# Sparse attention: projections as split products in one pass over the input, index scores of two heads side by side, index weights turned

## The reference, cut to what matters

```python
proj = h @ w_in                      # h: 512 x 1024, the normalised and modulated input
q = proj[..., :1024]                 # 16 heads of 64
ckv = _rmsnorm(proj[..., 1024:1152], kv_norm)     # latent, 128 wide
q_idx = proj[..., 1152:1664]         # 8 index heads of 64
k_idx = proj[..., 1664:1728]         # one index key of 64
w_idx = proj[..., 1728:] * (8 ** -0.5 * 64 ** -0.5)   # 8 weights a token
s = einsum('bthd,bsd->bths', q_idx, k_idx)
score = einsum('bth,bths->bts', w_idx, relu(s))   # causal; then the best 128 of each row
...                                  # attention over the selected latents, a bias by distance
```

## Time and profile before

| what | us |
|---|---|
| median of 3 runs | 2845.82 (2843.67 to 2848.26) |
| the profiled execution, own time | 2844.33 |
| its span, first to last instruction | 2842.5 |
| TensorE busy, share of span | 2707.7 (95%) |
| VectorE / ACT / POOL busy | 1369.2 / 1038.4 / 343.4 |
| mean granted TensorE clock | 0.978 |

### The profile page before, as it was taken

One profiled execution on the slowest core, in us unless ns is written; L12 is line 12 of the kernel. 1 busy time (PEld: TensorE's weight loads), 2 busy tenths in 40 slices (PEclk: granted clock), 3 DMA queues, 4 the chain that ended last, 5 costly groups with the idle time before them and its releaser, 6 DMA issues.

```text
span 2842.5 us, 46206 instructions
## 1 busy us (share of the span) xinstructions
PE 2707.7 (95%) x19024; PEld 2007.3 (71%) x19024; DVE 1369.2 (48%) x2302; ACT 1038.4 (37%) x1598; POOL 343.4 (12%) x268
## 2 busy tenths in 40 slices
PE   7999998899999989989999989999889999999999
PEld 4566666468888644577888868888677667788886
DVE  6566656253333337754333354433447676344335
ACT  5334333144432231744442243232223574333223
POOL 3232323010000101401000020000013131000000
PEclk9999999889999999999999989999989999999999
DMA  5344433322232112022223212232231002222231
GB/s 227 104 132 134 139 126 110 108 82 103 90 119 89 63 45 74 1 89 74 103 89 117 91 45 103 89 120 84 82 112 67 2 9 97 89 89 103 102 113 59
DMA packets 46585, 261.12 MB, mean 92 GB/s; under 512 B 5161, under 2 KB 7609, under 8 KB 26201
## 3 DMA queue, kind: packets, MB, share of 16 engines
q1 hardware_dynamic: 45416, 254.23, 25.8%
q10 hardware_dynamic: 1008, 4.57, 0.4%
HBM read 256.63 MB, written 2.15 MB: 91 GB/s over the span
## 4 chain that ended last, share of the span: by engine, by line
PE 89%; DVE 4%; ACT 3%; POOL 1%; issue 1%; DMA 1%; SPq 0%; DVEq 0%; ACTq 0%; POOLq 0%; PEld 0%; PEldq 0%
PE psum L220 87%; PE psum L2081 2%; DMA ada_first<-in_ada_first 1%; POOL ysum L568 0%; POOL branch_in L570 0%; DVE residual L1545 0%; ACT L614 0%; POOL join L563 0%; DVE weights L254 0%; DVE residual L1537 0%; ACT yg L648 0%; ACT ln_in L1500 0%; ACT nsa_probs L2117 0%; DVE Y_pairs L776 0%; DVE ln_stat L1529 0%
## 5 line engine op out<-in xcount | busy, mean ns | idle before, releaser
L220 PE MATMUL psum<-ffn_in_hi,ffn_weights_hi 128*128 128x512 f32 x848 | 339.9, 401 | 20.7 <-DVE ffn_in_lo L1652 8.4
L220 PE MATMUL psum<-ffn_in_lo,ffn_weights_hi 128*128 128x512 f32 x848 | 333.9, 394 | 0.0
L220 PE MATMUL psum<-ffn_in_hi,ffn_weights_lo 128*128 128x512 f32 x848 | 333.5, 393 | 0.0
L1674 ACT ACTIVATE ffn_weights_hi<-weights 128x1024 fp32r<-128x1024 f32 (+1 forms) x128 | 145.9, 1142 | 490.5 <-PE psum L220 490.5
L1674 ACT ACTIVATE ff_weights_hi<-weights 128x1024 fp32r<-128x1024 f32 (+1 forms) x120 | 137.7, 1147 | 433.3 <-PE psum L220 433.3
L220 PE MATMUL psum<-ff_in_hi,ff_weights_hi 128*128 128x512 f32 x704 | 277.5, 394 | 11.7 <-DVE ff_in_lo L1551 7.2
L1677 DVE TENSOR_TENSOR ff_weights_lo<-weights,ff_weights_hi 128x1024 fp32r<-128x1024 f32 (+1 forms) x116 | 156.0, 1345 | 253.8 <-ACT ff_weights_hi L1674 253.8
L220 PE MATMUL psum<-ff_in_lo,ff_weights_hi 128*128 128x512 f32 x704 | 276.2, 392 | 0.0
L220 PE MATMUL psum<-ff_in_hi,ff_weights_lo 128*128 128x512 f32 x704 | 276.1, 392 | 0.0
L1677 DVE TENSOR_TENSOR ffn_weights_lo<-weights,ffn_weights_hi 128x1024 fp32r<-128x1024 f32 (+1 forms) x126 | 166.9, 1327 | 110.5 <-ACT ffn_weights_hi L1674 110.5
L220 PEld LDWEIGHTS psum<-ffn_in_hi,ffn_weights_hi 128*128 128x128 f32 x848 | 161.7, 191 | 61.1 <-DVE ffn_weights_lo L1677 9.2
(11 more groups left out here) (560 smaller groups left out, 4865.3 us busy)
## 6 DMA issues: line engine op xcount, KB each, us to landing
weights<-in_ff_in SPq DMA_DIRECT2D x44, 1024.0 KB, 4.8
weights<-in_ffn_in SPq DMA_DIRECT2D x44, 1024.0 KB, 4.8
weights<-in_ada SPq DMA_DIRECT2D x80, 512.0 KB, 3.8
weights<-in_ff_out SPq DMA_DIRECT2D x16, 1408.0 KB, 6.0
weights<-in_ffn_out SPq DMA_DIRECT2D x16, 1408.0 KB, 6.1
weights<-in_rwkv SPq DMA_DIRECT2D x8, 1152.0 KB, 5.5
weights<-in_rwkv SPq DMA_DIRECT2D x8, 640.0 KB, 4.0
weights<-in_ada_first SPq DMA_DIRECT2D x4, 1024.0 KB, 11.4
```

Of the source, the lines that this page charges most:

```text
L220: return nc.tensor.matmul(out, lhsT, rhs, start=start, stop=stop)
L1674: return nc.scalar.activation(sp_.hi[u][:, 0:width], slot[s][:, u * width:(u + 1) * width], ACT.Copy)
```

## The change

- Input: the normalisation now writes both the full `attention_in` and its split parts, into the buffers that later hold the attention's output (`mixed`, seen as `h`).
- Weights: all projections become three split matmuls each. ACT rounds the weights (`first_hi` inside the normalisation, then `hi qi2`, `hi qi3`, `query_hi`), POOL subtracts (`first_lo`, `q_lo`). The rounded parts live in the output projection's weight buffers (`split`), in the probability buffer (`probs_rounded`) and in one new buffer.
- Order on TensorE: for the first four input tiles the latent and the index key; then index queries 0 and 1 over the same four; then for each of the last four tiles all four outputs.
- Index weights: eight weight columns against 512 moving columns, scaled by ACT, then turned by four small f32 matmuls and copied by VectorE.
- Scores: 12 steps of two products, one for each head, in the two halves of the rows and in two banks; one relu of both banks; two additions. The zeroing of the unused halves is gone.
- The bias product no longer waits for the latent. The first two queries come ahead of the bias windows, the other six behind them; SP's loads are reordered with them. The loop forms of the query stage are written out.
- The semaphores of several feed-forward stages (`gated_*`, `projected_pe`) are shared through `steps_again`, with a base added to the values waited for.

```diff
-        def steps_again(name, names):
+        def steps_again(name, names, turns=1):
...
-            in_turn[name] = s, base + 2 * len(names)
+            in_turn[name] = s, base + (turns + 1) * len(names)
...
+                def first_hi(act, u):
+                    if u == 0:
+                        hi_split.enter(act)
+                        act.wait_ge(*load_a.arrived())
+                        for name in ("ckv", "kidx"):
+                            hi, at = thirds[name]
+                            for n in range(2):
+                                last = nc.scalar.activation(hi[n][:, :], slot[0][:, at + n * T:at + (n + 1) * T], ACT.Copy)
+                            last.then_inc(*hi_split.step(name))
+                        return
+                    act.wait_ge(*load_b.arrived())
+                    for n, name in enumerate(("qi0", "qi1")):
+                        nc.scalar.activation(held[n], of_slot(slot, name), ACT.Copy).then_inc(*hi_split.step(name))
+                    nc.scalar.activation(small_weights[:, 0, :], small_raw, ACT.Copy).then_inc(*hi_split.step("widx"))
...
             def pool(pool):
-                pool.wait_ge(*reached(*branch[0]))
-                nc.gpsimd.memset(qi[:, :, :, :], 0.0).then_inc(zeroed, 1)
+                for name, n in (("qi2", 2), ("qi3", 3)):
+                    pool.wait_ge(*act_done(f"hi {name}"))
+                    nc.gpsimd.tensor_tensor(of_slot(slot_rounded, name), of_slot(slot, name), held[n].bitcast(F32), ALU.subtract).then_inc(
+                        *lo_split.step(name))
+                q_lo.enter(pool)
+                for j in range(KT):
+                    pool.wait_ge(*q_hi(f"hi{j % 2}", j // 2))
+                    nc.gpsimd.tensor_tensor(held[2 * (j % 2) + 1], query_raw(j), held[2 * (j % 2)].bitcast(F32), ALU.subtract).then_inc(
+                        *q_lo.step(f"lo{j % 2}"))
...
+                for k in range(4):
+                    pe.wait_ge(*reached(*branch[k]))
+                    for bank, name in enumerate(("ckv", "kidx")):
+                        if k == 0:
+                            pe.wait_ge(*lo_split(name))
+                        step(name, bank, k)
+                for bank, name in ((2, "qi0"), (3, "qi1")):
+                    pe.wait_ge(*lo_split(name))
+                    for k in range(4):
+                        step(name, bank, k)
+                for k in range(4, KT):
+                    pe.wait_ge(*reached(*branch[k]))
+                    for bank, name in ((0, "ckv"), (1, "kidx"), (2, "qi0"), (3, "qi1")):
+                        step(name, bank, k)
...
+                    last = three_of(ps[0:IH, 4, :], (small_weights[:, 0, w], small_weights[:, 1, w]), (h[0][:, k, :], h[1][:, k, :]),
+                                    k == 0, k == KT - 1)
...
-                pe.wait_ge(*dve_done("ckv"))
...
+                for q in range(QT):
+                    last = mm(ps[:, 4, q * IH:(q + 1) * IH], wide[:, q * P:(q + 1) * P], ident[0:IH, 0:IH])
+                last.then_inc(*pe_done.step("widx turned"))
...
-                    mm(ps[:, 6 + t % 2, 0:w], qi[:, m % 2, hh, q * P:(q + 1) * P], kidx[:, 0:w]).then_inc(*pe_done.step(f"score{t}"))
+                    for hh in range(2):
+                        r = slice(hh * HD, (hh + 1) * HD)
+                        last = mm(ps[:, SCORES[t % 2][hh], 0:w], qi[r, m % 2, q * P:(q + 1) * P], kidx[r, 0:w])
+                    last.then_inc(*pe_done.step(f"score{t}"))
...
+                def query(j):
+                    n, i = j % 2, j // 2
+                    pe.wait_ge(*q_lo(f"lo{n}", i))
+                    pe.wait_ge(*q_act(f"query{n}", i, 1))
+                    for k in range(KT):
+                        w = slice(k * P, (k + 1) * P)
+                        last = three_of(ps[:, n, :], (held[2 * n][:, w], held[2 * n + 1][:, w]), (h[0][:, k, :], h[1][:, k, :]), k == 0, k == KT - 1)
+                    last.then_inc(*q_pe.step(f"query{n}"))
+                query(0)
+                query(1)
+                pe.wait_ge(rows_in, 32)
+                pe.wait_ge(*act_done(f"relu{NI - 1}"))
+                for j in range(KT):
+                    if j >= 2:
+                        pe.wait_ge(near_copied, j - 1)
+                    mm(ps[:, 2 + j % 2, :], cc("flip"), windows[j]).then_inc(near_turned, 1)
+                for j in range(2, KT):
+                    query(j)
...
+                    nc.scalar.activation(rel[:, t % 2, :, 0:w], ps[:, b:b + 2, 0:w], ACT.Relu).then_inc(*act_done.step(f"relu{t}"))
```

More of the change, by code:

```diff
@@ L2226, in sparse_attention @@
             scratch = d["bias_scratch"]
[L2227 removed]
+            todo = [(m, q) for m in range(IH // 2) for q in range(1, QT)]
             NI = len(todo)
[L2229 to L2231 removed]
@@ L2232, in sparse_attention @@
-            act_done = steps("idx_act", ["ckv sq", "kidx", "qi0a", "qi0b", "ckv std", "far", "bias"]
-                          + [n for t, (m, hh, q) in enumerate(todo)
-                             for n in ([f"relu{t}"] + ([f"qi{m + 1}a", f"qi{m + 1}b"] if hh == 0 and q == 3 and m < 3 else []))])
-            dve_done = steps("idx_dve", ["widx", "ckv rstd", "ckv"] + [f"add{t}" for t in range(NI)] + [f"causal{q}" for q in range(1, QT)])
+            SCORES = ((6, 7), (4, 5))
+            pe_done = steps("idx_pe", ["ckv", "kidx", "qi0", "qi1", "ckv sq", "widx", "bias", "widx turned"]
+                         + [n for t, (m, q) in enumerate(todo) for n in [f"qi{m + 1}"] * (q == 1 and 1 <= m < 3) + [f"score{t}"]])
@@ L2236, in sparse_attention @@
+            act_done = steps("idx_act", ["ckv sq", "kidx", "qi0", "qi1", "ckv std", "widx", "far", "bias", "hi qi2", "hi qi3"]
+                          + [n for t, (m, q) in enumerate(todo) for n in [f"relu{t}"] + [f"qi{m + 1}"] * (q == 1 and 1 <= m < 3)])
+            dve_done = steps("idx_dve", ["ckv rstd", "ckv", "widx"] + [f"add{t}{hh}" for t in range(NI) for hh in range(2)]
+                             + [f"causal{q}" for q in range(1, QT)])
             topk_done = steps("top_dve", [f"max{q}" for q in range(1, QT)] + [f"take{q}" for q in range(1, QT)])
@@ L2326, in act @@
-                for t, (m, hh, q) in enumerate(todo):
+                nc.scalar.activation(brow[:, :], ps[0:16, 1, 0:BIAS_LEN], ACT.Identity, bias=far[:, :], scale=-1.0).then_inc(*act_done.step("bias"))
+                act.wait_ge(*load_c.arrived())
+                for n in (2, 3):
+                    nc.scalar.activation(held[n], of_slot(slot, f"qi{n}"), ACT.Copy).then_inc(*act_done.step(f"hi qi{n}"))
+                for t, (m, q) in enumerate(todo):
                     w = (q + 1) * P
@@ L2420, in pe_queries @@
-            def pe_queries(pe):
-                q_pe.enter(pe)
-                pe.wait_ge(*act_done("bias"))
-                with pe.Fori(0, KT // 2) as i:
-                    for s in range(2):
-                        pe.wait_ge(*q_loads[s].arrived(i))
-                        pe.wait_ge(*q_act(f"query{s}", i, 1))
-                        for k in range(KT):
-                            last = mm(ps[:, s, :], wtile(s, k), h[:, k, :], k == 0, k == KT - 1)
-                        last.then_inc(*q_pe.step(f"query{s}"))
@@ L2431, in act_queries @@
-            def act_queries(act):
-                q_act.enter(act)
-                with act.Fori(0, KT // 2) as i:
-                    for s in range(2):
-                        act.wait_ge(*q_pe(f"query{s}", i))
-                        alone(act)
-                        nc.scalar.activation(tile_of(qs, i * 2 + s), ps[:, s, :], ACT.Copy, scale=-HD ** -0.5).then_inc(
-                            *q_act.step(f"query{s}"))
-            phase(sp=sp_queries, pe=pe_queries, act=act_queries)
+            phase(sp=sp, pool=pool, pe=pe, act=act, dve=dve)
```

286 lines of the change are left out of this document (168 added, 118 removed).

## The result

The changed kernel takes 2812.63 us (median of 4 runs, 2804.41 to 2813.97), the kernel before 2847.04 in the same comparison: ratio 0.987 (95% interval 0.986 to 0.989), 34.4 us faster. The forecast was 2804, range 2797 to 2820: the time lies in the range, 8.6 us above the point, or 8.8 above the 2803.8 that was rounded to it. Of the 8.8, 2.7 are the base, since I counted from the profiled execution (2844.3) and the median of before is 2847.0 here; 6.1 are missing from the gain of 40.5. The profiled execution took 2811.76, its span is 2809.9, TensorE's mean granted clock 0.974 (before 0.978).

What follows compares the result with a forecast made beforehand. TensorE's chain was taken to bound the kernel. The attention's first addition moves from 1129.3 to 1086.4 + 1.5, 41.4 us, less 0.9 for the clock: 40.5 off 2844.3 gives 2803.8, stated as 2804, range 2797 to 2820.

Steps and rivals of the forecast that it cites:

- rival A: Top-k beside the queries: POOL's six subtractions hold it up by 14.1 us; gain 27, time 2817; chance 0.12.
- rival C: Whole changed part: split matmuls run at the 1.2 GHz level, 67 us more, time 2871; chance 0.02.
- rival B: Head pairs not side by side, or clock low through weights and index queries 2: gain 33 to 37; chance 0.18.
- the cover of 4.6 us: Queries: copy, split, subtraction and hand-overs between two uses of a buffer, 4.6 us, hide behind a 5.44 us product group.
- first split product: TensorE's start on the projections: at 976.6, +12.1 after ACT's last square, later than now but then without waits.
- Relu 0 to query 0: Index scores, from ACT's first relu to TensorE's first matmul of the first query: 20.0 us.
- the price of a product: All 112 projection products: three split matmuls at 0.2267 us instead of 0.859 a product, saving 0.179 each, 20.0 us.
- my step from the scores to MAX8: VectorE between the end of the scores at 1035.2 and the top-k's start at 1036.3: 1.1 us.
- The attention: Start of the attention: VectorE's add waits 1.5 us because masks of the second tile come later than TensorE.
- the terms behind the last score: TensorE from the last score at 1031.1 through queries, bias windows and copy: ends at 1083.5.
- The front: First projections: 96 split matmuls, 21.8 us, plus 2.5 for a low clock at their start; end at 1001.
- POOL's hold-up: Normalisation: VectorE steps with two SBUF inputs wait for POOL, 0.9 us to the first scaled tile, 1.3 behind it.

Runs made afterwards that it cites:

- e2: Changed kernel with GpSimd's second query-weight remainder waiting for the last causal mask, and query 1 moved behind the bias windows: 2811.2 us.
- e9: The changed kernel run once more, unaltered: 2812.5 us.
- e1: Changed kernel with split products in the sparse attention ordered hi x hi, hi x lo, lo x hi, so two share a stationary tile: 2810.3 us.
- e3: Changed kernel with the new stationary-tile order for every split product of the kernel and GpSimd's second query-weight remainder after the last causal mask: 2809.3 us.
- e8: Changed kernel with four extra f32 filler products behind the norm's last product, in TensorE's wait for the first projection input: 2806.6 us.
- e10: Changed kernel with the new stationary-tile order, the later GpSimd remainder and the four filler products together: 2805.38 us, ratio 0.9856.
- e11: Changed kernel with the new stationary-tile order in the sparse attention alone, run a second time: 2810.2 us.
- e6: Changed kernel with head pairs undone: each head again over 128 rows, its queries beside 64 rows of zeros: 2813.6 us.
- e7: Changed kernel with queries 2 to 7 multiplied in plain f32 as before the change, their rounding and remainders cut to one column: 2818.0 us.
- e12: Changed kernel with the later GpSimd remainder and the four filler products, without the new stationary-tile order: 2806.1 us.
- e4: Kernel before with only the shared semaphores of the feed-forward and projection stages: 2850.09 us (median of 10 runs), ratio 1.0007.
- e5: Changed kernel with GpSimd's remainders of the projections' weights cut to one column, TensorE multiplying by the rounded part instead: 2808.7 us.

## Why the prediction was right, and where its sizes were off

**Right in mechanism.** TensorE still sets the end; the selection ends with it and is not what holds; the top-k is untouched by POOL (rival A falls: 48.56 against 48.54); the pairs run side by side and the 144 matmuls of the front and of index queries 2 and 3 run mostly at full clock (rival C falls, and rival B in its two conditions, but for 3.4 us of low clock at the start of index queries 2); no effect of the shared semaphores shows; queries 2 to 7 never wait for POOL, so the cover of 4.6 us held; index weights took 0.2313 a matmul, 5.55 us for 24, against 5.4. The measured gain of 32.6 in the profiles and 34.4 in the medians is nevertheless nearer to the 33 to 37 of rival B than to the forecast's 40.5: it came from other terms, and the number alone would not have told the two apart.

**The working of the gain.** Forecast 40.5, profiled 32.6. By TensorE's chain, forecast against measured after the mark: first split product +12.1 and +12.39; relu 0 +46.6 and +46.70; query 0 +66.6 and +69.61; attention's first product +119.3 and +123.32. Against the kernel before, relu 0 comes 11.6 us earlier and MAX8 20.4; no run undoes the new order of the front or the turned index weights alone, so how much each of them gives is read from rows and not shown by an experiment. The terms that were off:
1. *Relu 0 to query 0*, 20.0 forecast, 22.9 measured. 1.6 of it is the clock at 1014 to 1017: with it (changed, e2, e9) the stretch takes 22.9, without it (e1, e3, e8, e10, e11) 21.3. The forecast had put 0.9 for it, at the end of its sum. Of the other 1.3, 0.3 is the pace of the 48 matmuls of index queries 2 and 3, and the pairs took 0.63 of the time of single heads where I had a half (6.0 saved for 7.7, e6). My own source had said so: 1.13 against 1.7 us in the earlier trace rows is 0.66. How much of that lies on the path the runs do not say.
2. *The pace of a split matmul*, 0.2267 in the step "the price of a product". It is 0.2333 here, 1.3 us over the 192 of the queries and some 2.1 over all 336 (the 96 at the front run at 0.232); a product saves 0.153 (e7), not 0.179, 17.2 us over 112. e1 excludes the order of the tiles. The input tiles are not it either: `attended` by the output projection's weights, at 1240 us of the kernel before, runs at 0.2267. Something about the weight tiles may be left, which no run tested; the cause stays open. The kernel before has both paces too, 0.2333 in its `mix_out` projection near 2380 us. My single row was a sample of one place.
3. *The causal masks*, 1.1 us in my step from the scores to MAX8, 3.15 measured. POOL's remainder of query 1 lay on them. It cost the time nothing, since TensorE was later (e2).
4. *The attention*, +2.25 us instead of 1.5. e8, with masks as late as in the changed kernel and the clock full through the stage, needs 90.71, 1.3 more than before; e3, e10 and e12, with masks 2 us earlier and a full clock, 89.7; e7, whose masks are long ready, 89.38, as before. So the masks' lateness was priced rightly at 1.3 for 1.5, and 0.9 is a stretch of low clock, granted 0.67 and 0.76 in the six microseconds from 1098; e1, e2, e9 and e11 have that stretch too and need 91.2 to 91.8.
5. *Outside the part*, nothing forecast, 4.0 measured: 1.7 ahead of it and 2.3 behind. It goes with the granted clock, which scatters: in the same code the executions need 962.95 to 969.14 ahead of it and 1622.0 to 1629.8 behind, and the kernel before was at the short end of both (964.46, 1623.9; e4, whose part is that of before, 970.81 and 1624.1). Where the changed kernel loses, the trace shows longer stretches of low clock: behind the part they add up to 76.0 us, against 62.5 before. Whether the change has a share in that is not settled: before and e4 both have 62.5 us at the low level there, and of the 12 profiles with the changed part two have the same (e7 and e12, with 1624.0 and 1622.0 us) and ten have 69 to 80, with 1625.2 to 1629.8. Behind the compressed blocks near 2110 us, before:

```profile
2117.00:2120.00 3.00, 3.00 (x13) 2.44 (x12) 0.82 (x4) 1.27 (x2) 0.95 (x1) 0.86 0.00 0
2120.00:2123.00 3.00, 3.00 (x15) 2.49 (x14) 0.00 (x0) 0.67 (x2) 1.45 (x1) 1.00 0.24 35
```

and the same work in the changed kernel:

```profile
2081.00:2084.00 3.00, 3.00 (x8) 2.32 (x8) 0.82 (x4) 1.87 (x3) 0.58 (x2) 0.50 0.00 0
2084.00:2087.00 3.00, 3.00 (x11) 2.35 (x11) 0.00 (x0) 0.00 (x0) 2.05 (x1) 0.76 0.00 0
```

Sum: 40.5, less 4.0 at TensorE (0.1 up to relu 0, 2.9 to query 0, and 1.0 from there, about the pace of the 192 matmuls of the queries), less 0.75 in the attention, less 4.0 outside, plus the 0.9 that was already taken off: 32.6. Two slips in the working are small: the rows give 48.54 us for the top-k where I wrote 48.4, and the terms behind the last score add up to 1083.3 where I wrote 1083.5.

**Two terms that agreed by luck.** The front got 2.5 us for a low clock behind the first split product. With a full clock throughout (e10) that stretch is no shorter (34.56 from first product to relu 0, against 34.31): TensorE then waits for VectorE's tiles instead, 1.5 us in three waits. The low clock's price lies ahead of it, in the norm's last product (2.07 instead of 1.12) and in what follows: VectorE's first remainder then meets POOL's second whole subtraction (2.64 us, 1.29 where the clock is full), and 12.4 becomes 10.1. And POOL's hold-up was forecast with 0.9 us up to the first scaled tile, which was met (+7.05 against +7.3), and 1.3 behind it. There it cost 2.0, all of it in the first remainder (L1555, 2.64 us for 0.68), and whether it does depends on the fast or slow product above. The additions and the masks got no such term in the sum at all. The Trainium skill, "SBUF — State Buffer", section Who interferes with whom, states an exclusive lock: a VectorE instruction with two SBUF inputs contends with a GpSimd instruction that reads SBUF, one with at most one SBUF input, outside the two-port modes, does not. The prediction named this rule for the sums and did not price it there. e5 bears it out for the first remainder, the spread, the additions and the masks (2.64, 1.28, 2.46 and 2.71 us back to 0.68, 0.69, 0.48 and 0.69), and the top-k's one-input steps are free, as it says (48.56 us with six subtractions beside them, 48.54 with none).

## What to carry to other kernels

When a stage is shortened, list every two-input VectorE step that lies beside a long GpSimd instruction and check which of them is on the path: here one remainder cost 2 us and was, three masks cost 2 us and were not. Take the price of a matmul from several places of the trace and carry their spread as a bound. If a short phase with little TensorE work precedes a dense one, a few useless products in its gap are worth a try, and the marks must say what they did: here four gave 2.9 us inside the part in one profile (e8) and 0.1 in another (e10 beside e3).

## What I had not expected of the hardware

- Two paces of the same split matmul at full granted clock, 0.2267 and 0.2333 us, by place, not by order.
- With a handful of f32 products in a 5.5 us gap, the granted clock was full in the index scores some 35 us later (0.50 at 1014 to 1017 in the changed kernel, 1.00 in e8). Profiles without them show both.
- The clock at one product of 1.1 or 1.9 us moves the next stage by 2.3 us, through an overlap of two other engines.
- Two heads on 64 rows each take 0.63 of the time of two on 128 rows one after the other (2.53 against 4.03), not half, although their records start 0.01 us apart.
- A VectorE step that started 0.94 us earlier fell into the first of two GpSimd subtractions instead of the second, and took 1.29 us instead of 2.64.
